# Stationary weight tiles interleaved in pairs: each 128-column tile is read with a step of 8 bytes

## The reference, cut to what matters

```python
# first block, two layers
h = h + mamba2_mixer(rmsnorm(h, g0), ...)        # w_in 1024 x 5152, w_out 2048 x 1024
h = h + conv_glu_ffn(rmsnorm(h, g1), ...)        # u = h @ w_up (1024 x 5632); (silu(conv(u1)) * u2) @ w_down
h = h + fox_attention(rmsnorm(h, g2), ...)       # w_in 1024 x 4112, w_out 1024 x 1024
h = h + conv_glu_ffn(rmsnorm(h, g3), ...)
h = rmsnorm(h, g)
# second block, 16 meta tokens in front
h = h + concat(mla_group(...), conv_group(...)) @ w_out
# peer_ffn: every token picks 8 x 16 of 16384 experts; the kernel computes all of them:
act = gelu(u_tab @ h.T);  h = h + (gates * act).T @ v_tab     # both tables 16384 x 1024
h = rmsnorm(h, g_final)
```

## Time and profile before

| | us |
|---|---|
| median of 3 runs | 1766.61 |
| lowest, highest run | 1755.48, 1771.8 |
| span of the profiled execution | 1774.7 |
| PE busy (share of the span) | 1710.5 (96%) |
| PEld busy | 1606.4 (91%) |
| DVE, ACT, POOL busy | 1044.9, 826.9, 900.8 |

### The profile page before, as it was taken

The page is one execution under the profiler, slowest core; times in us unless marked ns, Lnnn a source line. Parts: engine busy times, 40 slices in busy tenths (PEclk is TensorE's granted clock), DMA queues, the critical chain, the costliest instruction groups (busy, mean ns, idle before and its releaser), DMA issues. The chain is left out here.

```text
span 1774.7 us, 34933 instructions
## 1 busy us (share of the span) xinstructions
PE 1710.5 (96%) x12583; PEld 1606.4 (91%) x12583; DVE 1044.9 (59%) x2198; ACT 826.9 (47%) x1147; POOL 900.8 (51%) x275
## 2 busy tenths in 40 slices
PE   8899799999999999999998999999999999999997
PEld 8889799999997999999678999999999978888886
DVE  7857654345344554344885891745555377777776
ACT  4578343334547433345435544644444443333332
POOL 4676468887682378876205588776666500000000
PEclk9999999999998999999988999999999999999999
DMA  5443335555452245554202466665555687777774
GB/s 212 143 144 118 113 126 190 190 188 192 143 190 72 72 167 190 188 183 160 93 1 84 164 234 236 210 205 177 178 177 177 216 266 240 240 241 243 239 242 160
DMA packets 77453, 310.79 MB, mean 175 GB/s; under 512 B 8768, under 2 KB 10304, under 8 KB 60736
## 3 DMA queue, kind: packets, MB, share of 16 engines
q1 hardware_dynamic: 75024, 306.14, 51.3%
q10 hardware_dynamic: 2352, 3.59, 0.6%
HBM read 290.82 MB, written 18.87 MB: 175 GB/s over the span
## 5 line engine op out<-in xcount | busy, mean ns | idle before, releaser
L759 POOL TENSOR_TENSOR lo<-raw,hi 128x2048 fp32r<-128x2048 f32 x127 | 584.3, 4610 | 378.1 <-ACT hi L584 306.0
L362 PE MATMUL ps<-xc,hi 128*128 128x256 f32 x1912 | 544.3, 285 | 5.7 <-DVE ps L2052 3.3
L363 PE MATMUL ps<-xcl,hi 128*128 128x256 f32 x1912 | 536.3, 280 | 0.0
L364 PE MATMUL ps<-xc,lo 128*128 128x256 f32 x1912 | 536.1, 280 | 0.0
L362 PEld LDWEIGHTS ps<-xc,hi 128*128 128x128 f32 x1912 | 362.6, 190 | 8.6 <-issue 6.9
L798 POOL TENSOR_TENSOR lo<-raw,hi 128x1024 fp32r<-128x1024 f32 x128 | 304.7, 2404 | 128.8 <-ACT hi L1767 128.7
L363 PEld LDWEIGHTS ps<-xcl,hi 128*128 128x128 f32 x1912 | 364.3, 191 | 0.1
L1767 ACT ACTIVATE hi<-raw 128x1024 fp32r<-128x1024 f32 x256 | 264.9, 1058 | 211.3 <-PE ps L364 199.0
L364 PEld LDWEIGHTS ps<-xc,lo 128*128 128x128 f32 x1912 | 360.6, 189 | 0.0
L2472 DVE TENSOR_TENSOR lo<-raw,hi 128x1024 fp32r<-128x1024 f32 x128 | 156.4, 1222 | 81.1 <-ACT hi L1767 81.0
L362 PE MATMUL ps<-hi,wgh 128*128 128x512 f32 x512 | 199.4, 389 | 1.8 <-DVE wgl L2483 1.8
(11 more groups left out here) (497 smaller groups left out, 3426.6 us busy)
## 6 DMA issues: line engine op xcount, KB each, us to landing
raw<-in_w_u SPq DMA_DIRECT2D x128, 512.0 KB, 4.3
raw<-in_w_v SPq DMA_DIRECT2D x128, 512.0 KB, 4.2
raw<-in_w_up SPq DMA_DIRECT2D x44, 1024.0 KB, 4.8
raw<-in_w_down SPq DMA_DIRECT2D x22, 1024.0 KB, 4.7
raw<-in_w_fox SPq DMA_DIRECT2D x16, 1024.0 KB, 5.0
act_save<-act_out SPq DMA_DIRECT2D x64, 256.0 KB, 2.1
act_in<-act_save SPq DMA_DIRECT2D x64, 256.0 KB, 3.2
raw<-in_w_xbc SPq DMA_DIRECT2D x12, 1024.0 KB, 5.0
```

The costliest lines, as they stand in the source:

```text
L362: pe.matmul(o, ah, bh, start=start, stop=False)
L363: pe.matmul(o, ah, bl, start=False, stop=False)
L364: return pe.matmul(o, al, bh, start=False, stop=stop)
L759: return g.tensor_tensor(lo[slot][:], raw[slot][:], hi[slot][:].bitcast(F32), ALU.subtract)
```

## The change

The columns of two neighbouring tiles of 128 are laced: where a unit held tile A (128 columns) and then tile B, it now holds A0 B0 A1 B1 and so on. This is done to the arrays on the host, before the kernel is launched (`laced`). The matmuls that take such weights as the stationary operand name every second column, so a tile's load reads 128 float32 with a step of 8 bytes out of 1024 bytes, instead of 512 neighbouring bytes. The second tile of a pair starts 4 bytes behind the first. In `pe_w` tiles c and c+1 (c even) are a pair, in the U half-units k and k+1.

Laced are the weights that are stationary: `w_xbc`, `w_sout`, `w_fout`, `w_conv`, `w_mout`, `w_wq`, `w_u`, `w_up`, `w_down`. Not laced are those that move (`w_z`, `w_fox`, `w_lat`, `w_v`). Every engine has as many instructions as before, in the same order, with the same waits; sizes and places of transfers and buffers are the same.

```diff
@@ pe_a
-                m = three(pe, outs[f], wh[:, k, f * P:(f + 1) * P], wl[:, k, f * P:(f + 1) * P],
+                m = three(pe, outs[f], wh[:, k, f::2], wl[:, k, f::2],
                           xh_[:, k, :], xl_[:, k, :], k == 0, k == KC - 1)
@@ pe_w
-        wh = hi[s][:].rearrange("p (a b) -> p a b", a=2)
-        wl = lo[s][:].rearrange("p (a b) -> p a b", a=2)
+        wh = hi[s][:].rearrange("p (a b two) -> p a b two", a=2, two=2)
+        wl = lo[s][:].rearrange("p (a b two) -> p a b two", a=2, two=2)
         for c in range(KC):
+            q = slice(c // 2 * P, (c // 2 + 1) * P)
...
-                m = three(pe, o, wh[:, kk, c * P:(c + 1) * P], wl[:, kk, c * P:(c + 1) * P], bh[:, kk, :], bl[:, kk, :],
+                m = three(pe, o, wh[:, kk, q, c % 2], wl[:, kk, q, c % 2], bh[:, kk, :], bl[:, kk, :],
...
@@ first_unit (its loads of wh, wl in the same way)
-                pe.matmul(ps[:, 0, 0:SEQ], wh[:, k, 0:P], xc[:, k, :], start=k == 0, stop=False)
+                pe.matmul(ps[:, 0, 0:SEQ], wh[:, k, 0::2], xc[:, k, :], start=k == 0, stop=False)
...
@@ u_half
-                wh, wl = cv3(hi[s][:, q]), cv3(lo[s][:, q])
+                wh = hi[s][:, q].rearrange("p (k c two) -> p k two c", k=KC // 2, two=2)
+                wl = lo[s][:, q].rearrange("p (k c two) -> p k two c", k=KC // 2, two=2)
...
-                    mm = three(pe, ps[:, s, f * SEQ:(f + 1) * SEQ], wh[:, k, :], wl[:, k, :],
+                    mm = three(pe, ps[:, s, f * SEQ:(f + 1) * SEQ], wh[:, k // 2, k % 2, :], wl[:, k // 2, k % 2, :],
                                xc[:, k, :], xcl[:, k, :], k == 0, k == KC - 1)
@@ kernel (host)
+    def laced(w):
+
+        return w.reshape(*w.shape[:-1], -1, 2, P).swapaxes(-2, -1).reshape(w.shape)
...
-        "w_xbc": by_columns(xbc), "w_z": by_columns(z), "w_sout": by_rows(a["ssd_w_out"][0]),
+        "w_xbc": by_columns(laced(xbc)), "w_z": by_columns(z), "w_sout": by_rows(laced(a["ssd_w_out"][0])),
...
-        "w_u": u, "w_v": vt, "gfin": a["g_final_2"][None],
+        "w_u": laced(u), "w_v": vt, "gfin": a["g_final_2"][None],
...
-        arrays[f"w_up{l}"] = by_columns(paired(a["ffn_w_up"][l], 2816))
-        arrays[f"w_down{l}"] = by_rows(a["ffn_w_down"][l])
+        arrays[f"w_up{l}"] = by_columns(laced(paired(a["ffn_w_up"][l], 2816)))
+        arrays[f"w_down{l}"] = by_rows(laced(a["ffn_w_down"][l]))
```

More of the change, by code:

```diff
@@ L853, in first_unit @@
                     pe.wait_ge(x_ready, k // 2 + 1)
-                pe.matmul(ps[:, 0, 0:SEQ], wh[:, k, 0:P], xc[:, k, :], start=k == 0, stop=False)
-                pe.matmul(ps[:, 0, 0:SEQ], wh[:, k, 0:P], xcl[:, k, :], start=False, stop=False)
+                pe.matmul(ps[:, 0, 0:SEQ], wh[:, k, 0::2], xc[:, k, :], start=k == 0, stop=False)
+                pe.matmul(ps[:, 0, 0:SEQ], wh[:, k, 0::2], xcl[:, k, :], start=False, stop=False)
             pe.wait_ge(lo_done, 1)
             for k in range(KC):
-                pe.matmul(ps[:, 0, 0:SEQ], wl[:, k, 0:P], xc[:, k, :], start=False, stop=k == KC - 1)
+                pe.matmul(ps[:, 0, 0:SEQ], wl[:, k, 0::2], xc[:, k, :], start=False, stop=k == KC - 1)
             for k in range(KC):
@@ L861, in first_unit @@
                     pe_squares(pe, 0, True, True)
-                m = three(pe, ps[:, 0, SEQ:2 * SEQ], wh[:, k, P:2 * P], wl[:, k, P:2 * P], xc[:, k, :], xcl[:, k, :],
+                m = three(pe, ps[:, 0, SEQ:2 * SEQ], wh[:, k, 1::2], wl[:, k, 1::2], xc[:, k, :], xcl[:, k, :],
                           k == 0, k == KC - 1)
@@ L2579 @@
         "x_t": a["x"][0].T.reshape(KC, P, SEQ).transpose(1, 0, 2), "cols": cols, "rows": rows, "w_dt": small(w_dt), "w_f": small(fox[:, 4096:]),
-        "w_xbc": by_columns(xbc), "w_z": by_columns(z), "w_sout": by_rows(a["ssd_w_out"][0]),
-        "w_fox": by_columns(fox[:, :4096]), "w_fout": by_rows(a["fox_w_out"][0]),
-        "w_conv": by_columns(paired(w2[:, :1024], 512)), "w_lat": by_columns(lat),
-        "w_mout": by_rows(a["w_out_2"][0]), "w_wq": by_columns(a["peer_wq_2"][0]),
+        "w_xbc": by_columns(laced(xbc)), "w_z": by_columns(z), "w_sout": by_rows(laced(a["ssd_w_out"][0])),
+        "w_fox": by_columns(fox[:, :4096]), "w_fout": by_rows(laced(a["fox_w_out"][0])),
+        "w_conv": by_columns(laced(paired(w2[:, :1024], 512))), "w_lat": by_columns(lat),
+        "w_mout": by_rows(laced(a["w_out_2"][0])), "w_wq": by_columns(laced(a["peer_wq_2"][0])),
         "w_uq": a["w_uq_2"][0].reshape(2, P, -1).transpose(1, 0, 2), "w_ukv": a["w_ukv_2"][0],
         "meta_t": a["meta_2"].T.reshape(KC, P, META).transpose(1, 0, 2), "cs": cs, "keys": a["peer_keys_2"][0].transpose(1, 3, 0, 2),
-        "w_u": u, "w_v": vt, "gfin": a["g_final_2"][None],
+        "w_u": laced(u), "w_v": vt, "gfin": a["g_final_2"][None],
     }
     for l in range(2):
-        arrays[f"w_up{l}"] = by_columns(paired(a["ffn_w_up"][l], 2816))
-        arrays[f"w_down{l}"] = by_rows(a["ffn_w_down"][l])
+        arrays[f"w_up{l}"] = by_columns(laced(paired(a["ffn_w_up"][l], 2816)))
+        arrays[f"w_down{l}"] = by_rows(laced(a["ffn_w_down"][l]))
     arrays = {k: np.ascontiguousarray(v) for k, v in arrays.items()}
```

## The result

The changed kernel takes 1796.26 us (median of 4 runs, 1795.26 to 1798.44) against 1767.0 (4 runs, 1755.48 to 1771.8): the ratio is 1.0168, with a 95% interval of 1.0128 to 1.0209. It is slower by some 29 us; I had forecast 24 us less. The time lies inside the range, on the wrong side. The profiled executions are 18.8 us apart, 1774.7 and 1793.5; why the medians are further apart is taken up with the experiments.

A forecast was written before the change was run, and what follows sets the result against it. PE, busy 96% of 1774.7 us, was taken as the bound; savings of 16.8, 3.4 and 5.0 us (25.2), less 1.5, gave about -24 us: 1751 profiled, 1743 us on the median's scale. The 8-in-10 range was 1730 to 1815.

The forecast's parts named there:

- The bound: Whole kernel: PE, busy 96% of 1774.7 us, sets the end by how closely matmuls follow each other.
- three readings of spacing: Matmuls with 256 moving columns: steady at 113.3 (moving side's limit) or 117.7 ns; 111.6 ns for an undisturbed load of neighbouring columns.
- The 6.6 ns beside the columns: Moving side: overhead of streaming per matmul, 73.3 ns for 160 columns against 66.7, and 106.7 + 6.6 = 113.3 for 256.
- The cause given to 117.7: Slow stretches: the load, disturbed by the moving side's reads, takes 6.1 ns more than its undisturbed 111.6 ns.
- the choice of the lower end for the laced load: 7776 laced loads: nearly all at 113.3 ns, saving 25.2 us before 1.5 taken off; chance 0.43.
- not out of reach: Laced load's rate: memory already delivers 8 neighbouring bytes per 0.83 ns to the moving side, with 6.6 ns to spare per matmul.
- two readers of equal speed part and stay parted: Laced load and moving side: with a step of 8 bytes both advance alike, so one no longer overtakes the other repeatedly.
- Rival A: All laced loads: the step doesn't matter, a stream's starting phase chooses the spacing; 1767 us, from 1743 to 1776; chance 0.29.
- Rival B: All 7776 laced loads: disturbed twice as often, 123.8 ns each, +57 us, 1824 us; chance 0.24 including its milder form.
- its milder form: Laced loads: the two readers meet once, then stay parted, at 118 to 121 ns; 1778 to 1802 us.
- rival C: Laced loads: reading every second word halves the load's rate, some 218 ns each, +790 us; chance 0.04.
- The unlaced matmuls: The 1152 matmuls with stationary tokens: not laced but may fall into the other spacing, 5 us either way.

The follow-up runs named there:

- streams_1: Bare matmul streams, not the model: load step 4 to 32 bytes and tile start varied; under 256 columns step 8 gave 119.9 to 121.2 ns, step 16 236 ns.
- streams_2: Bare matmul streams kept at full clock, varying load step, load columns and moving columns; under 160 moving columns step 4 gave 111.7 ns, step 8 117.9.
- place64: Kernel before, nothing laced, buffers raw, hi and lo starting 64 instead of 128 bytes past a multiple of 256; 1806.79 us against 1765.56, ratio 1.0241.
- u_by_four: Kernel before with only table U laced in fours, its 3072 loads read with a step of 16 bytes; 2124.48 us in one run.
- streams_3: Bare matmul streams varying load steps, grouping of moving columns and starts; about 1.8 ns per 16-byte piece; loads of 16 columns gave 113.1 and 117.9 ns.
- streams_4: Bare streams of 36 contiguous loads under 256 moving columns, thirteen kinds of small matmuls between them, nine times each; 4.49 us after two, 4.35 after three.

## Why the prediction was wrong, point by point

**The bound, and the three readings of spacing, held.** PE sets the end, no other engine came near, nothing was late next. 113.3, 117.7 and 111.6 ns were read rightly and came back in bare streams. That nothing lasts between the first two holds for this kernel's places: at others, step 4 gave a steady 116.7 (streams_1, L98). The 106.7 and 66.7 ns of the prediction are 256 and 160 moving columns at 0.417 ns each, and this is the rate that rows 5 and 6 give, (113.3 - 73.3) / 96. The 6.6 ns beside the columns are an estimate from those two rows; under 320 moving columns the spacing was 146.8 ns (streams_2, L163), 13.5 above 320 x 0.417.

**The cause given to 117.7 was wrong.** I put it down to a disturbed load. Streams with loads of only 16 columns have both spacings, 113.1 and 117.9. My reason, that 512 columns show nothing of it, held only for the place they have in this kernel: elsewhere they take 233.4 (place64).

**The step that failed is the choice of the lower end for the laced load**, and in it the sentence that the moving side shows the rate to be "not out of reach". The row was the right one and I read it the wrong way. The moving side reads 1024 bytes of a partition in 113.3 ns, which is 6.6 more than 256 x 0.417. A laced load reads the same 1024 bytes, 64 pieces, and has, as an estimate, its own fixed 4.9 ns beside: 111.6 less 106.7, which is 128 columns at 0.833 ns; the load records give 0.84 ns a column (188 ns for 128 columns, 94 for 16, streams_2, L163 and L193). An estimate from those two rows alone would have been 113.3 + 4.9 = 118.2 ns; measured 117.9. This sum is made after the fact and is not a shown mechanism: at 96 pieces it gives 171.1 + 4.9 = 176.0 where 173.3 was measured. What is shown is the floor: with 118 for the load, 113.3 can't be reached in any phase. 120.0 instead of 116.8 over some 7576 spacings is 23 to 24 us, where the forecast had -25.2.

**How much of the result that step explains.** From the forecast 113.3 to the measured 120.0 ns are 6.7 ns; the load's own time, 117.8 ns, makes 4.5 of them. Against the 116.8 ns of the profile before it is 1.0 of 3.2 ns, some 8 of the 23 us. So the load's own time alone turns the forecast gain into a loss, but the larger part of the loss, 2.2 ns or some 17 us, comes on top of it, and its cause stays open.

**The other argument for it, that two readers of equal speed part and stay parted, fell too.** Laced streams under 256 columns are at 119.9 to 121.2 in all starts and places tried, 2 ns or more above the load alone. What makes these 2 ns was not found.

**Rival A** (the step doesn't matter) is refuted for the step, but its observation was the better half of my text: a phase does choose between 113.3 and 117.7, and three small matmuls set it. **Rival B** had the sign, and its milder form the size (118 to 121 ns, 1778 to 1802 us); its mechanism, one meeting of the two readers, is not what puts 113.3 out of reach, since 117.9 stands under 160 moving columns, but it may be behind the 2.2 ns on top: under 160, 192, 224 and 256 moving columns step 8 gave 117.9, 118.3, 118.6 and 120.0, and under 512 lacing cost 6.6 ns on the moving side. No run tells the meeting from another cause. Its full form (124 ns) and **rival C** (218 ns) did not occur; a price of C's size comes with a step of 16 bytes. The chance of slower by over 1% was 0.26.

**The unlaced matmuls** stayed within the 5 us allowed for their phase: with stationary tokens 116.3 ns before, 117.5 after, 1.4 us in 1133 spacings.

**The unit of 16 bytes.** Streams and kernel agree on it. With two elements of the load in each piece of 16 bytes the load is a little longer, 117.9 against 111.7 ns with four (streams_2, L73 and L68). With fewer the price is large: 173 ns with one and a third (step 12, streams_2, L158), 235.5 with one (step 16, streams_1, L178), and 233 in table U of u_by_four.

**A load's time does not follow from its columns alone.** For 128 columns the loads took 111.7 to 244 ns by their step, and place64 lost 2.4% by addresses only, and lacing the load slowed a stream of 512 moving columns from 226.7 to 233.3 ns. So for these float32 tiles the time does not go with the columns alone, and what the load reads is felt on the moving side.

## What to carry to other kernels

Count what a load or a stream touches in 16-byte pieces of each partition, beside its columns, and compare with the other side of the same matmul: here 64 pieces cost 118 ns, and a stream whose two sides stand at 111.6 and 113.3 has no room for the step. When a trace holds a reader that already touches as much of the same memory, price the new access by its whole time, and do not count what it needs over its columns as time to spare. And when the same instructions show two steady spacings in one trace, expect the median to wander with them, and compare kernels in several runs rather than profile against profile.

## What the runs showed of the hardware that I had not expected

- At the places of this kernel, a stream of matmuls with 256 moving columns of this type has two steady spacings, 113.3 and 117.8 ns, chosen by its start. The fast one was kept over 300 matmuls in a bare stream (streams_3, L183), the slow one over nearly 1450 in the kernel before (266.1 to 436.6 us, 117.8 ns on average); two small matmuls ahead of it gave the slow one in nine cases of nine, three the fast one (streams_4).
- The place modulo 256 bytes of stationary against moving tile is worth 2.4% of this kernel: 1806.8 against 1765.6 us.
- A load's price by pieces is not on TensorE's clock: at a granted clock of 0.50 a step of 16 bytes took 233.3 ns, at 1.00 under 256 columns 235.5 (streams_1), and a stream with a step of 20 bytes went from 224 to 226.7 as its clock fell from 1.00 to 0.50 (streams_3, L93), while loads with a step of 4 bytes went from 111.7 to 213.3 (streams_1, L68).
- The moving side pays by the same pieces: 256 columns in pairs 16 bytes apart took 227 to 229 ns, in fours 32 bytes apart 116 (streams_3, L108 and L103).
- Lacing the load can slow the moving side: under 512 moving columns, both tiles 128 bytes past a multiple of 256, the spacing went from 226.7 to 233.3 ns (streams_2, L238 and L243) although the load, 117.9 ns under 160 columns, has over 100 ns to spare.
